# Attention index scores: 32 queries of four heads as one stationary operand, and the sum over heads in four column tiles

## The reference, cut to what matters

```python
# iq: (tokens, 8 heads, 64), ik: (tokens, 64), iw: (tokens, 8); blocks of 128 queries
s = jnp.einsum('bqhd,bsd->bqhs', iqb, ikf)
idx_score = jnp.einsum('bqhs,bqh->bqs', jax.nn.relu(s), iwb * w_scale)
idx_score = jnp.where(causal[None], idx_score, NEG_INF)
_, sel = lax.top_k(idx_score, n_sel)          # n_sel = 256
# logits of the selected keys, softmax over them, times v, for 6 heads of 128
```

## Time and profile before

| | |
|---|---|
| median of 3 runs | 5257.47 us |
| the profiled execution, span from first to last instruction | 5248.9 us |
| PE busy | 4773.0 us, 91% |
| DVE busy | 3065.1 us, 58% |
| ACT busy | 1841.8 us, 35% |
| POOL busy | 977.8 us, 19% |

### The profile page before, as it was taken

One profiled execution on the slowest core, in us unless ns is written; L12 is line 12 of the kernel. 1 busy time (PEld: TensorE's weight loads), 2 busy tenths in 40 slices (PEclk: granted clock), 3 DMA queues, 4 the chain that ended last, 5 costly groups with the idle time before them and its releaser, 6 DMA issues. The chain is left out here.

```text
span 5248.9 us, 68534 instructions
## 1 busy us (share of the span) xinstructions
PE 4773.0 (91%) x23705; PEld 3529.8 (67%) x23759; DVE 3065.1 (58%) x4877; ACT 1841.8 (35%) x2663; POOL 977.8 (19%) x1073
## 2 busy tenths in 40 slices
PE   7999678889999976589999999999999999999977
PEld 3444334444444433378999999999999999999822
DVE  2222278888888885356565755475675566755522
ACT  1111123333333332144443544353454344543400
POOL 0000122121111111121121211121121211211155
PEclk9999789999999988789999999999999999999988
DMA  4332211000000000065555655465565455654455
GB/s 183 115 115 107 84 27 27 14 19 22 14 14 18 12 12 8 21 220 175 180 170 180 205 183 169 160 205 175 179 219 192 168 197 179 223 192 152 149 193 184
DMA packets 426875, 663.73 MB, mean 126 GB/s; under 512 B 22080, under 2 KB 286272, under 8 KB 425696
## 3 DMA queue, kind: packets, MB, share of 16 engines
q1 hardware_dynamic: 367920, 507.46, 29.4%
q0 software_dynamic: 26576, 85.56, 4.6%
q10 hardware_dynamic: 32256, 69.22, 3.4%
HBM read 542.86 MB, written 119.31 MB: 126 GB/s over the span
## 5 line engine op out<-in xcount | busy, mean ns | idle before, releaser
L1371 PE MATMUL gu<-x_hi,w_hi 128*128 128x256 f32 (+2 forms) x4096 | 1230.9, 301 | 1.3 <-DVE x_lo L1453 1.3
L1372 PE MATMUL gu<-x_lo,w_hi 128*128 128x256 f32 (+2 forms) x4096 | 1231.6, 301 | 0.0
L1373 PE MATMUL gu<-x_hi,w_lo 128*128 128x256 f32 (+2 forms) x4096 | 1228.8, 300 | 0.0
L1448 DVE TENSOR_TENSOR w_lo<-w_raw,w_hi 128x2048 fp32r<-128x2048 f32 x386 | 874.5, 2286 | 532.7 <-ACT w_hi L1522 532.7
L1522 ACT ACTIVATE w_hi<-w_raw 128x2048 fp32r<-128x2048 f32 x386 | 726.9, 1907 | 282.9 <-PE gu L1373 195.9
L1371 PEld LDWEIGHTS gu<-x_hi,w_hi 128*128 128x128 f32 x4096 | 772.1, 189 | 2.5 <-issue 1.7
L1373 PEld LDWEIGHTS gu<-x_hi,w_lo 128*128 128x128 f32 x4096 | 773.1, 189 | 0.0
L1372 PEld LDWEIGHTS gu<-x_lo,w_hi 128*128 128x128 f32 x4096 | 770.0, 188 | 0.7
L1344 POOL TENSOR_TENSOR a_lo<-up,a_hi 128x384 fp32r<-128x384 f32 x256 | 396.9, 1550 | 1488.3 <-ACT a_hi L1534 1488.3
L1371 PE MATMUL yp<-w_hi,a_hi 128*128 128x512 f32 x1296 | 526.3, 406 | 0.0
L1372 PE MATMUL yp<-w_lo,a_hi 128*128 128x512 f32 x1296 | 515.2, 398 | 0.0
(11 more groups left out here) (258 smaller groups left out, 5582.9 us busy)
## 6 DMA issues: line engine op xcount, KB each, us to landing
w_raw<-w_gate_up SPq DMA_DIRECT2D x258, 1024.0 KB, 7.6
w_raw<-w_down SPq DMA_DIRECT2D x128, 1024.0 KB, 6.2
y_dram<-y_rows ACTq DMA_DIRECT2D x192, 256.0 KB, 3.2
y_dram<-zeros SPq DMA_DIRECT2D x16, 2016.0 KB
h_blk<-h_dram SPq DMA_DIRECT2D x32, 512.0 KB, 5.4
qi_dram<-qi_stage ACTq DMA_DIRECT2D x16, 640.0 KB, 2.9
w_in_sb<-w_in SPq DMA_DIRECT2D x1, 8480.0 KB, 24.1
x_in<-x SPq DMA_DIRECT2D x16, 512.0 KB, 9.2
```

Of the source, the lines that this page charges most:

```text
L1371: nc.tensor.matmul(out, s_hi_, m_hi, start=(n == 0), stop=False)
L1372: nc.tensor.matmul(out, s_hi_, m_lo, start=False, stop=False)
L1373: op = nc.tensor.matmul(out, s_lo_, m_hi, start=False, stop=(n == len(pairs) - 1))
L1448: nc.vector.tensor_tensor(w_lo[:, c % 2, cols], raw[:, c % 3, cols], w_hi[:, c % 2, cols].bitcast(F32), ALU.subtract).then_inc(s_lo, 1)
```

## The change

Index queries are stored in another order: `stage[:, slot, 6:10]` now holds, for a group g of 32 queries, the four head pairs one after the other, so that `iq[rows, b % 2, g]` has 128 columns that stand for 32 queries of four heads (the even heads in partitions 0 to 63, j = 0, the odd ones in 64 to 127, j = 1). One unit (g, j) of product is 128 rows (head, query) by up to 512 keys, and there are eight units, as there were eight heads. The sum over heads of a unit is a matmul with a stationary operand of 128 rows and 32 columns, `w_sum[:, g, j]`, and its result goes to the 32 partitions of `acc` that belong to group g. Four sums, one for each g, are issued in a row, by `UNITS`; a group's second sum adds to the first.

For `w_sum`, weights have to stand by (head, query) in the partitions. Each tile's `iw` is stored to a new DRAM tensor `iw_dram` in the projection stage (ScalarE's queue), and SyncE loads it turned at the head of the attention stage: four transfers of 32 x 64 pieces of two floats. GpSimd builds the eight operands of a block in one instruction of 128x256 in place of eight of 128x128. There are four ReLU buffers in place of three.

```diff
@@ project_stage, out_of_q
-                    nc.scalar.activation(stage[:, slot, 6:10], tr[:, 1], ACT.Copy).then_inc(s_qi, 1)
+                    nc.scalar.activation(
+                        stage[:, slot, 6:10].rearrange("p a n -> p (a n)").rearrange("p (g c q) -> p c g q", g=4, c=4),
+                        tr[:, 1].rearrange("p c (g q) -> p c g q", g=4), ACT.Copy).then_inc(s_qi, 1)
...
+                    nc.scalar.dma_start(D_["iw"][bass.ds(t * P, P), :], S["iw"][:, t]).then_inc(s_iwst, 16)
@@ attend_stage
+    RELUS = 4
+    CUT = 2 * P // IDX_H
+    CUTS = P // CUT
+    UNITS = ((0, 0), (1, 1), (2, 0), (3, 1), (1, 0), (0, 1), (3, 0), (2, 1))
@@ sync
+                for c in range(IDX_H // 2):
+                    sp.dma_start(iw_turned[c * CUT:(c + 1) * CUT].rearrange("q b g j -> q (b g) j"),
+                                 D_["iw"][:, 2 * c:2 * c + 2].rearrange("(n q) j -> q n j", q=CUT),
+                                 allow_slow_non_contiguous=True).then_inc(s_iw, 16)
                 load_q(0)
@@ gpsimd
                 def prepare(b):
                     wait(pool, s_wsum, IDX_H * chunk0[b])
-                    for i in range(IDX_H):
-                        op = nc.gpsimd.tensor_scalar(w_diag[:, i], S["ident"][:], S["iw"][:, b, i:i + 1], 1.0,
-                                                     ALU.mult, ALU.mult)
-                    op.then_inc(s_wd, 1)
+                    shape = [P, CUTS * 2, CUT]
+                    nc.gpsimd.tensor_tensor(w_sum[:].rearrange("p g j q -> p (g j) q"),
+                                            same_row[:].unsqueeze(1).broadcast_to(shape),
+                                            iw_turned[:, b].rearrange("p g j -> p (g j)").unsqueeze(2).broadcast_to(shape),
+                                            ALU.mult).then_inc(s_wd, 1)
...
+                pool.wait_ge(s_iw, 16 * IDX_H // 2)
                 prepare(2)
@@ tensor
-                    for j in range(2):
+                    for g, j in UNITS[i:i + 2]:
                         rows = slice(IDX_D * j, IDX_D * (j + 1))
-                        nc.tensor.matmul(pair[:, j, 0:width], iq[rows, b % 2, i // 2],
+                        nc.tensor.matmul(pair[:, j, 0:width], iq[rows, b % 2, g],
                                          S["ikT"][rows, at:at + width], start=True, stop=True).then_inc(s_idx, 1)
+
+                def weigh_units(b, c, i):
+
+                    u = IDX_H * (chunk0[b] + c) + i
+                    width = min(BANK, keys[b] - c * BANK)
+                    pe.wait_ge(s_relu, u + CUTS)
+                    for n, (g, j) in enumerate(UNITS[i:i + CUTS]):
+                        nc.tensor.matmul(acc[g * CUT:(g + 1) * CUT, 0:width], w_sum[:, g, j],
+                                         relu[:, (u + n) % RELUS, 0:width], start=(i == 0), stop=(i > 0)
+                                         ).then_inc(s_wsum, 1)
@@ tensor, score
-                    for i in range(0, IDX_H, 2):
-                        if i + 2 < IDX_H:
-                            index(b, c, i + 2)
-                        else:
-                            pe.wait_ge(s_relu, u0 + IDX_H)
-                        for j in (i, i + 1):
-                            nc.tensor.matmul(acc[:, 0:width], w_diag[:, j], relu[:, (u0 + j) % 3, 0:width],
-                                             start=(j == 0), stop=(j == IDX_H - 1)).then_inc(s_wsum, 1)
+                    index(b, c, 2)
+                    index(b, c, 4)
+                    weigh_units(b, c, 0)
+                    index(b, c, 6)
+                    weigh_units(b, c, CUTS)
@@ scalar, score
-                        wait(act, s_wsum, u0 + i - 2)
-                        nc.scalar.activation(relu[:, (u0 + i) % 3, 0:width], pair[:, i % 2, 0:width],
+                        wait(act, s_wsum, u0 + i - RELUS + 1)
+                        nc.scalar.activation(relu[:, (u0 + i) % RELUS, 0:width], pair[:, i % 2, 0:width],
                                              ACT.Relu).then_inc(s_relu, 1)
```

More of the change, by code:

```diff
@@ L639, in _ @@
                 nc.gpsimd.memset(so_far[:], 0.0)
+                nc.gpsimd.memset(same_row[:], 0.0)
                 nc.gpsimd.memset(before[:], 1.0)
@@ L651, in _ @@
                                         base=0, pattern=[[1, P]], channel_multiplier=-1)
+                for c in range(P // CUT):
+                    nc.gpsimd.affine_select(out=same_row[:], in_=same_row[:], compare_op=ALU.not_equal, fill=1.0,
+                                            base=-c * CUT, pattern=[[-1, CUT]], channel_multiplier=1)
+                    pool.drain()
                 for b in range(2):
```

14 lines of the change are left out of this document (9 added, 5 removed).

## The result

The changed kernel takes 5264.18 us (median of 8 runs, 5255.42 to 5274.46), the kernel before 5255.48 us beside it (8 runs, 5250.83 to 5257.82): a ratio of 1.0023, with a 95% interval of 1.0013 to 1.0033. That is 9 us slower, where the forecast had 2.9 us faster. So the loss is small, 9 to 14 us of 5255, and real: both intervals leave out 1. Medians and ratios here leave out three executions, at 5600 to 8382 us, in which the chip was in a slower state.

What follows compares the result with a forecast made beforehand. VectorE was taken to set the pace in the attention stage. Terms -6.3 - 7 + 4 + 0.4 (projection-stage stores) + 6 gave -2.9 us, a median of 5254.6 us, no change; 8 in 10: 5232 to 5296.

Steps and rivals of the forecast that it cites:

- What bounds the kernel: Attention stage, 1060 to 1860 us: VectorE sets the pace; TensorE's gain can be cashed only in 49.6 us of waits.
- The chunk on TensorE: A 512-key chunk falls from 10.9 to 9.7 us: four sums take 1.1 us, three holes of 1.2 to 1.7 open.
- Rival 1: Index sums on TensorE: the four column tiles do not run together; about 5272 or 5310 us; chance 0.15.
- What it is worth, -6.3 us: Shorter chunk 0 where VectorE waits behind it: 5.4 us, plus 0.9 in block 0; range 0 to -45.
- TensorE's clock, +6: Slow stretches ahead of the mask in three more blocks, 1 us each, and half a dozen chunks 0, 0.5 each.
- Rival 2: Slow stretches inside TensorE's chunks: the holes cost the clock, +24 us with a third hit, about 5279; chance 0.18.
- GpSimd, -7: 2.1 us less ahead of the scatter; a third of TensorE's 23.5 us waiting for r_diag counts; range 0 to -20.
- The start, +4: VectorE's first maximum comes later through four loads ahead in the queue: issues and small pieces; range 0 to +20.
- Rivals 3 and 4: 3: TensorE is the real bound, -25, about 5230, chance 0.2. 4: only the loads reach the path, chance 0.12.
- rival 4: Only the loads reach the path, GpSimd's saving being swallowed by the scatter's landing; 5258 to 5268 us; chance 0.12.
- wrong if: Signs against: four sums 2 us or more, clock below 0.93, waits behind chunks 1 and 2, attention over 15 us shorter.

Runs made afterwards that it cites:

- e6_fill0: Changed kernel with spare products, whose results are unused, in the three TensorE holes of chunk 0 alone; 5249.1 us, 0.9995 of the kernel before.
- e2_pairs: Changed kernel with sums two units at a time, each pair behind the next pair of products, still in column tiles; 5244.7 us, 0.9984 of the kernel before.
- e3_exp4: Changed kernel with ScalarE's exponential ahead of ReLU 4 in place of ReLU 6; 5276.9 us, 1.0046 of the kernel before.
- e9_many: Changed kernel with GpSimd making w_sum eight times over in each block; 5306.7 us, 1.0096 of the kernel before.
- e7_serial: Changed kernel with units reordered so that four sums go to two column tiles, two each, in place of four; 5262.2 us, 1.0017 of the kernel before.
- e14_scatter: Changed kernel with GpSimd's preparation of w_sum and its scatter moved behind the values that end the block; 5255.5 us, 1.0000 of the kernel before.
- e5_start: Kernel before with only the change's 16 iw stores and four turned loads ahead of all others; 5260.1 us, 1.0014 of the kernel before.

## Why the prediction was wrong

**What bounds the kernel**: right in the main. VectorE sets the pace, and what counts is what it waits for: `e6_fill0`, `e2_pairs`, `e3_exp4` and `e9_many` move the time with these waits, not with TensorE's busy time (81 us less of it, and slower). Two readings of the waits were off. Those not at head 0 were said to be mostly at head 2; it is 6.4 of 13.1 us, and head 1 has 5.4. And the largest wait behind GpSimd, 12.2 us at the end of block 2, was missing from the 50.5 us.

**The chunk on TensorE**: right in every part, the 1.06 us of a group, the three holes, 9.3 us against 9.7. Rival 1 did not happen, and `e7_serial` shows that its price was wrong as well: two by two costs nothing against four, not the 18 us worked out.

**What it is worth, -6.3 us**: this step failed. It took a chunk 0 that is 1.2 us shorter for logits that are 1.2 us earlier, and priced the logits behind it at the old clock. They start 0.9 us earlier in block 13 and end later, because their own records double. The term's sign is wrong: where 5.3 us of waits ahead of head 2 in blocks 8, 9, 11, 12 and 13 should have fallen to nearly none, they rose by 8.5 us; over blocks 5 to 13 they rose from 6.7 to 14.1 us in one trace and to 14.3 in the other. Block 0's part, 0.9 us, came in the faster trace alone. With chunk 0 filled, so that the clock holds, the term has the right sign: these waits are 1.2 us.

**TensorE's clock, +6**: the right mechanism at too small a size, and at the wrong place. I charged slow stretches inside the chunks and ahead of the mask at 0.5 to 1 us each; what meets VectorE is the group of 4 to 5 us that follows chunk 0. No run measures this term and the one before together. An estimate is the total, less the start, plus the saving on GpSimd: between 9 - 6 + 7 and 14 - 3 + 12, so +10 to +23 us, where the forecast had 0 net. Filling chunk 0 gives 15 to 20 back. Rival 2 names this cause (0.18); its 5279 is 10 to 15 us too slow, and it prices the products and sums inside the chunk at the low level, which happens too (`e7_serial`, block 0), but not the logits behind it. I held against it that the clock was 0.96 "with many pauses"; that was the clock of a kernel whose sums ran 3.86 us without a pause ahead of these logits, which is the very thing that the change removes.

**GpSimd, -7**: right sign, and the size at the low end of the 7 to 12 measured, but not for the reason given. The wait for `r_diag` fell by 8.3 us, from 23.5 to 15.2, and `e14_scatter` gains 9 to 14 us from 11.1 us less of it: nearly all of this wait counts, not a third. Its largest piece, 9.5 of the 23.5 us, stands at the end of block 2, where the mask is ready long before. That the term came out near its size is luck.

**The start, +4**: 3.0 us at the first maximum (1.7 to 4.6 over the traces), 6.3 in the median of `e5_start` with an interval that holds both; the 0.42 us of an issue was too low for these loads (0.9).

Rivals 3 and 4 did not come: nothing of TensorE's freed time was cashed, and the change does reach the path. The number 5264.18 lies in rival 4's 5258 to 5268 and, barely, in the forecast's own 5246 to 5265, but by the mechanism of neither: a loss behind chunk 0 and a gain on GpSimd happen to leave a small sum. The conditions written down as "wrong if" caught it: the clock in 1060 to 1860 is 0.90, below 0.93, and the waits for `qk` there rose.

One number under the forecast was read wrongly. The 8.6 us between the profiled span and the median were put down to what lies outside the span. In the changed kernel's profiled execution 1.6 us lie outside it (5255.42 against 5253.8); the rest is that the profiled execution of the kernel before was among its faster ones (its eight run from 5250.83 to 5257.82).

## What to carry to other kernels

Where one engine waits for a group of matmuls, price the group at the clock that the work ahead of it leaves behind: a shorter stretch with holes can deliver later than a longer one without, and a few spare products in the holes tell in one run whether that is so. Keep independent matmuls spread between the steps of another engine rather than bunched, even if bunching makes them cheaper. An idle engine's microsecond is not free either: look at what queues behind it (here the scatter's landing ahead of `r_diag`), and reorder that first.

## What the runs showed of the hardware

- Four float32 sums of 128 rows, 32 columns and 512 keys take 1.06 us in four column tiles, 1.92 us in two, and 3.86 us as full 128x128 operands: 3.6 times as fast, where I had only two tiles to go by.
- At TensorE's low level matmuls take nearly twice as long: 2.05 us in place of 1.10 for two records of 512 columns, 2.08 in place of 1.13 for the four records of a pair of products.
- A one-column VectorE instruction with two inputs in the core's memory stood still for up to 2.2 us while a GpSimd tensor_tensor ran (all 30 in `e2_pairs` end within 0.02 us of a GpSimd instruction's end), and 128x1920 instructions with one input did not (2.21 us with and without). The other way round, in the changed kernel three `r_diag` instructions on GpSimd took 3.46 us, where each usually takes 0.37: the second took 2.00 while VectorE ran a 128x1664 instruction with two inputs, the third 1.13 while it wrote the mask, with one:

```profile
1633.79 3.46 POOL L698 TENSOR_SCALAR r_diag<-ident,small 128x128 f32<-128x128 f32 x3 [9.59 <-DMA lists_dram<-token,at_i]
...
1634.02 1.89 DVE L775 SCALAR_TENSOR_TENSOR scores_even<-mask,scores_even 128x1664 f32<-128x1664 bf16 x1
```

- SyncE needs 0.9 us to issue a transfer of 2048 pieces of 8 bytes, and the load queued behind it 1.55 us, where an ordinary issue takes 0.42.
